# Gate and up projections in seven half-size products per pair, and the down projection in a stage of its own

## What is computed

```python
    x = x + gt1 * (merged @ w_out)                      # w_out 1024 x 1024
    h2 = rmsnorm(x, g_ffn) * (1 + sc2) + sh2            # sc2, sh2, gt2: one row per group of tokens
    gate, up = jnp.split(h2 @ w_gu, 2, axis=-1)         # w_gu 1024 x (2 * 2816)
    x = x + gt2 * ((jax.nn.silu(gate) * up) @ w_down)   # w_down 2816 x 1024
    return x, new_hist, C1, n1, m1
...
    y_prompt = rmsnorm(xp, g_final)
    y_sample = rmsnorm(xs, g_final)
```

## Time and profile before

| | us |
|---|---|
| median of 3 runs | 2039.96 (2039.92 to 2041.27) |
| the profiled execution | 2040.03 |
| its span, first to last instruction | 2038.3 |
| TensorE busy | 1975.2 (97%) |
| VectorE busy | 757.2 (37%) |
| ScalarE busy | 464.0 (23%) |
| GpSimd busy | 147.4 (7%) |
| DMA, mean | 99 GB/s |

### The profile page before, as it was taken

One profiled execution on the slowest core, in us unless ns is written; L12 is line 12 of the kernel. 1 busy time (PEld: TensorE's weight loads), 2 busy tenths in 40 slices (PEclk: granted clock), 3 DMA queues, 4 the chain that ended last, 5 costly groups with the idle time before them and its releaser, 6 DMA issues.

```text
span 2038.3 us, 28505 instructions
## 1 busy us (share of the span) xinstructions
PE 1975.2 (97%) x11613; PEld 1880.7 (92%) x11613; DVE 757.2 (37%) x1332; ACT 464.0 (23%) x656; POOL 147.4 (7%) x251
## 2 busy tenths in 40 slices
PE   7999999999999999999999969999999999999997
PEld 4899999999999987778999959999999999999997
DVE  5422213213333432334534554432442343344246
ACT  4232212223343342222202012111111111111113
POOL 0010029010000013210000011000000000000000
PEclk9999999999999999999999979999999999999999
DMA  8653335432434347445432311111111111111112
GB/s 284 240 170 114 120 109 163 145 112 77 117 100 123 102 144 166 134 143 186 152 98 65 101 36 32 42 52 41 41 41 51 41 41 41 43 50 41 41 52 88
DMA packets 224146, 200.84 MB, mean 99 GB/s; under 512 B 13251, under 2 KB 202487, under 8 KB 224079
## 3 DMA queue, kind: packets, MB, share of 16 engines
q1 hardware_dynamic: 214958, 166.31, 27.4%
q10 hardware_dynamic: 7721, 29.25, 3.6%
q0 software_dynamic: 1408, 4.46, 0.8%
HBM read 150.19 MB, written 49.92 MB: 98 GB/s over the span
## 4 chain that ended last, share of the span: by engine, by line
PE 94%; DVE 3%; ACT 1%; DMA 1%; issue 1%; SPq 0%; DVEq 0%; ACTq 0%
PE dense L1765 80%; PE misc L2075 2%; PE misc L2062 1%; PE misc L2001 1%; PE misc L2005 1%; PE misc L1974 1%; PE dense L1848 1%; PE misc L2003 1%; PE misc L1895 1%; PE misc L1894 1%; PE misc L1984 1%; DVE act_lo L1215 1%; PE misc L1848 1%; PE misc L2174 0%; DVE stage L1208 0%
## 5 line engine op out<-in xcount | busy, mean ns | idle before, releaser
L1765 PE MATMUL dense<-act_hi,w_hi 128*128 128x384 f32 (+1 forms) x2808 | 646.4, 338 | 19.7 <-DVE act_lo L1215 16.7
L1765 PE MATMUL dense<-act_lo,w_hi 128*128 128x384 f32 (+1 forms) x2808 | 622.1, 329 | 0.0
L1765 PE MATMUL dense<-act_hi,w_lo 128*128 128x384 f32 (+1 forms) x2808 | 621.0, 329 | 0.0
L1765 PEld LDWEIGHTS dense<-act_hi,w_hi 128*128 128x128 f32 x2808 | 481.1, 189 | 44.8 <-issue 27.7
L1765 PEld LDWEIGHTS dense<-act_hi,w_lo 128*128 128x128 f32 x2808 | 482.3, 189 | 0.0
L1765 PEld LDWEIGHTS dense<-act_lo,w_hi 128*128 128x128 f32 x2808 | 482.0, 189 | 0.0
L1200 DVE TENSOR_TENSOR w_lo<-raw,w_hi 128x1024 fp32r<-128x1024 f32 x139 | 173.0, 1245 | 464.5 <-ACT w_hi L821 463.7
L821 ACT ACTIVATE w_hi<-raw 128x1024 fp32r<-128x1024 f32 x139 | 146.9, 1058 | 397.9 <-PE dense L1765 395.7
L1697 DVE SCALAR_TENSOR_TENSOR hmT<-dense,mod,hmT 128x768 f32<-128x768 f32 x80 | 81.4, 1018 | 69.1 <-PE dense L1765 68.6
L926 ACT ACTIVATE stage<-dense 128x768 f32<-128x768 f32 x52 | 42.1, 810 | 285.1 <-PE dense L1765 285.0
L1765 PE MATMUL dense<-a_lo,w_hi 128*128 128x384 f32 (+1 forms) x480 | 106.3, 329 | 0.0
(11 more groups left out here) (302 smaller groups left out, 1486.7 us busy)
## 6 DMA issues: line engine op xcount, KB each, us to landing
z_scratch<-stage ACTq DMA_DIRECT2D x52, 544.0 KB, 2.7
raw<-in_w_in_dram SPq DMA_DIRECT2D x53, 512.0 KB, 3.8
ada_w<-in_w_ada_dram SPq DMA_DIRECT2D x24, 1024.0 KB, 5.5
raw<-in_w_gate_up_dram SPq DMA_DIRECT2D x44, 512.0 KB, 3.7
stage<-z_scratch SPq DMA_DIRECT2D x24, 544.0 KB, 3.6
raw<-in_w_down_dram SPq DMA_DIRECT2D x22, 512.0 KB, 3.5
qkv<-z_scratch SPq DMA_DIRECT2D x8, 1024.0 KB, 6.9
cs<-in_state_mlstm_c_dram SPq DMA_DIRECT2D x32, 256.0 KB, 5.3
```

What stands on the lines that cost most here:

```text
L1765: ins = pe.matmul(tile(k, c), w[:, n % 2, off:off + P], x[:, xr, t0:t1], start=(first and p == 0), stop=(last and p == 2))
```

## The change

**Gate and up.** The T = 1088 tokens are cut into two halves of TH = 544 (the second holds 480 prompt and the 64 sample tokens), the 1024 features into two halves of four tiles, and the output rows into gate and up. The product of these two by two blocks is made with seven products of half-size blocks (steps 0 to 6, STEPS), not eight, and 15 sums (Strassen's form in Winograd's variant): four of weight blocks (w_sums), four of activation blocks (combine, once for the whole stage), and the rest of results. Two hidden tiles are worked on together as a *pair*, 11 pairs (DUOS); each step has one product for each of the two tiles (q). A product is 4 feature tiles x 3 passes x 2 chunks of 272 columns = 24 matmuls, and a pair has 14. Two of the four sets of two PSUM banks serve a tile; steps 3 to 6 add onto what stands in the bank, and ScalarE copies out what other steps left (take_s1, take_s5, take_s2), VectorE adds to it (add_g1, add_g2, add_u2), and forms silu(gate) * up (gate2 for the second half of tokens, gate1 for the first). Weights are split by half blocks of 512 columns through a ring of four (w_high, w_low). The result is stored to DRAM (a_scratch, 22 x 544 KB).

**The norm** before it is made by token half. The last two units of the output projection run half by half; the first half's norm sums (col_sums, spread) stand between the second half's matmuls, the second half's between the first products of gate and up. GpSimd takes no part.

**Down** is a stage behind all of gate and up: six phases, for each token chunk (320, 384, 384) the first and the last 512 output features, in each 11 units of 24 matmuls over 256 hidden rows, into four banks. w_down is loaded and split three times over, through a ring of four (66 x 512 KB); the activations are loaded again from a_scratch and split, one chunk while the one before is used; x is stored to DRAM before the FFN and loaded again (8 x 544 KB) for the sum. The final norm goes by halves of 512 features.

The core of the diff:

```diff
+HT = 5
+KH = KT // 2
+KB = KH * P
+DUOS = FT // 2
+STEPS = 7
+DN, DQ = 2 * STEPS, 2
+IN_X, FRESH = (0, 3, 5, 6), (0, 1, 2)
+LOOP0, LOOPS = 3, 3
...
+        OPS = [tuple(blocks(ap) for ap in pair_) for pair_ in (
+            (first_op(0), first_op(1)), (first_op(2), first_op(3)), (half_op(2), half_op(3)), (half_op(0), half_op(1)),
+            (half_op(6), half_op(7)), (half_op(4), half_op(5)), (last_op[:, 0, :], last_op[:, 1, :]))]
...
+        def w_src(d, st, q):
+            g, u = raw_pair(d, q)
+            tmp = ssq[:, 0:KB] if d == 0 and q else s1b
+            return (g[:, 0:KB], g[:, KB:2 * KB], tmp, g[:, 0:KB], g[:, KB:2 * KB], u[:, 0:KB], u[:, KB:2 * KB])[st]
...
+        def p_banks(st, q):
+            return bank_pair(q if st in IN_X else 2 + q)
...
+            def gu_load(d, sem_, value, i=0):
+                for up in range(2):
+                    for q in range(2):
+                        src = gu_cols(d, q, up, i)
+                        if (up, q) == (0, 0):
+                            sp.wait_ge(sem_, value)
+                        sp.dma_start(raw_pair(d, q)[up].rearrange("p (k n) -> p k n", k=KT), src
+                                     ).then_inc(gu_in[(d - 1) % 2], 16)
+            def a_store(d, i=0):
+                for q in range(2):
+                    dst = a_rows(d, q, i)[:, TH:T]
+                    sp.wait_ge(a2_ready, at(d, DQ, q + 1, i))
+                    sp.dma_start(dst, sums[:, 2 + q, :]).then_inc(a2_out, 16)
+                for q in range(2):
+                    dst = a_rows(d, q, i)[:, 0:TH]
+                    sp.wait_ge(a1_ready, at(d, DQ, q + 1, i))
+                    sp.sem_inc(passed, 1)
+                    sp.dma_start(dst, set_sums(d, q)).then_inc(a1_out[d % 2], 16)
...
+                    if v == 3:
+                        sp.wait_ge(alo_ready, UNITS)
+                        sp.wait_ge(wlo_ready, DN * DUOS)
+                        for o in range(KT):
+                            sp.dma_start(hmT[:, o, :], z[Z_X + o]).then_inc(x1_in, 16)
...
+                if d or st > 2:
+                    act.wait_ge(p_done, at(d, DN, e - 3, i))
+                elif st:
+                    act.wait_ge(oh_full, 2 + st)
+                act.activation(w_ops(d, st, q)[0], w_src(d, st, q), ACT.Copy).then_inc(whi_ready, 1)
...
+            def take_s1(d, q, i=0):
+                act.wait_ge(p_done, at(d, DN, q + 1, i))
+                if d >= 2:
+                    act.wait_ge(a1_out[d % 2], i * 32 + 32 * (d // 2))
+                elif d:
+                    act.wait_ge(hlo_ready, HLO0 + 4 * KH)
+                act.activation(two(set_sums(d, q)), p_banks(0, q), ACT.Copy).then_inc(s1_ready, 1)
...
+            def w_sums(d, q, i=0, part=None):
+                g, u = raw_pair(d, q)
+                a11, a12, a21, a22 = g[:, 0:KB], g[:, KB:2 * KB], u[:, 0:KB], u[:, KB:2 * KB]
+                t = w_src(d, 2, q)
+                n = at(d, 8, 4 * q, i) if part is None else 3 * q
+                if part != 1:
+                    if part is None:
+                        dve.wait_ge(wlo_ready, at(d, DN, 4 + q, i))
+                    dve.tensor_tensor(t, a21, a22, ALU.add).then_inc(wsum_ready, 1)
+                    dve.wait_ge(wsum_ready, n + 1)
+                    dve.tensor_tensor(a21, a11, a21, ALU.subtract).then_inc(wsum_ready, 1)
+                    dve.wait_ge(wsum_ready, n + 2)
+                    dve.tensor_tensor(a11, t, a11, ALU.subtract).then_inc(wsum_ready, 1)
+                if part != 0:
+                    dve.wait_ge(wsum_ready, n + 3 if part is None else 6)
+                    dve.tensor_tensor(a12, a12, a11, ALU.subtract).then_inc(wsum_ready, 1)
...
+            def combine(st, kt):
+                first, second = hmT[:, kt, :], hmT[:, kt + KH, :]
+                dst, x, y = {2: (first[:, 0:TH], first[:, TH:T], first[:, 0:TH]), 3: (t2(kt), second[:, TH:T], first[:, 0:TH]),
+                             5: (first[:, TH:T], second[:, TH:T], first[:, TH:T]),
+                             6: (second[:, 0:TH], second[:, 0:TH], t2(kt))}[st]
+                if st < 4:
+                    dve.wait_ge(hs32_ready, HS0 + KT + KH * (st - 2) + kt + 1)
+                dve.tensor_tensor(dst, x, y, ALU.subtract).then_inc(hlo_ready, 1)
...
+            def add_g1(d, q, i=0):
+                dve.wait_ge(p_done, at(d, DN, DQ + q + 1, i))
+                dve.wait_ge(s1_ready, at(d, DQ, q + 1, i))
+                sa = two(set_sums(d, q))
+                dve.tensor_tensor(sa, p_banks(1, q), sa, ALU.add).then_inc(g1_ready, 1)
...
+            for k in range(6):
+                residual(k)
+            half_residual(6, 0)
+            for q in range(2):
+                w_low(0, 0, q)
+            half_residual(7, 0)
+            wait_full(dve, raw_in, U_FFN + 1, inc=16)
+            w_sums(0, 0, part=0)
+            half_diag(0)
+            dve.wait_ge(gu1_in, 32)
+            w_sums(0, 1, part=0)
+            half_residual(6, 1)
+            dve.wait_ge(rstd_ready, RSTD0 + 1)
+            dve.wait_ge(x1_out[0], 16 * KT)
+            for k in range(KH + 1):
+                if k < KH:
+                    norm_half(k, k, 0, TH)
+                if k:
+                    plain_low(k - 1)
+            for q in range(2):
+                w_low(0, 1, q)
+            half_residual(7, 1)
+            sum_h2(6)
+            sum_h2(7)
+            norm_half(4, 4, 0, TH)
+            norm_half(5, 5, 0, TH)
+            plain_low(4)
+            half_diag(1)
+            norm_half(6, 6, 0, TH)
+            plain_low(5)
+            norm_half(7, 7, 0, TH)
+            plain_low(6)
+            plain_low(7)
+            dve.wait_ge(wsum_ready, 6)
+            for q in range(2):
+                w_sums(0, q, part=1)
+            for q in range(2):
+                w_low(0, 2, q)
+            dve.wait_ge(rstd_ready, RSTD0 + 2)
+            dve.wait_ge(x1_out[1], 16 * 2)
...
+            made(2, add_g1s)
+            for q in range(2):
+                w_low(0, 3, q)
+            made(3)
+            for q in range(2):
+                w_low(0, 4, q)
+            made(4)
+            for q in range(2):
+                w_low(0, 5, q)
+            made(5)
+            for q in range(2):
+                add_g2(0, q)
+            for q in range(2):
+                w_low(0, 6, q)
+            made(6)
+            for q in range(2):
+                add_u2(0, q)
+            for q in range(2):
+                w_low(1, 0, q)
+            for q in range(2):
+                gate2(0, q)
+            gate1(0, 0)
...
+                gate1(d - 1, 1, i)
+                for q in range(2):
+                    w_low(d, 1, q, i)
+                w_sums(d, 0, i)
+                w_low(d, 2, 0, i)
+                w_sums(d, 1, i)
+                w_low(d, 2, 1, i)
+                add_g1(d, 0, i)
+                add_g1(d, 1, i)
+                for q in range(2):
+                    w_low(d, 3, q, i)
+                groups(0, 1)
+                for q in range(2):
+                    w_low(d, 4, q, i)
+                groups(2, 3)
+                for q in range(2):
+                    w_low(d, 5, q, i)
+                add_g2(d, 0, i)
+                add_g2(d, 1, i)
+                groups(4, 5)
+                for q in range(2):
+                    w_low(d, 6, q, i)
+                add_u2(d, 0, i)
+                add_u2(d, 1, i)
+                gate2(d, 0, i)
+                gate2(d, 1, i)
+                if not last:
+                    for q in range(2):
+                        w_low(d + 1, 0, q, i)
+                groups(6, 7)
+                gate1(d, 0, i)
...
-            pe.wait_ge(xsum_ready, 1)
-            col_sums(R_N2, ssq)
-            pe.wait_ge(diag_ready, 2)
-            sum_partitions(T_N2, sq)
...
+            wait_full(pe, round_free, R_NOUT)
+            half_unit(6, 0)
+            half_unit(7, 0)
+            half_unit(6, 1, 0, 4)
+            col_sums(0)
+            half_unit(6, 1, 4)
+            half_unit(7, 1, 0, 4)
+            spread(0)
+            half_unit(7, 1, 4)
+            def product(d, st, q, i=0):
+                pe.wait_ge(wlo_ready, at(d, DN, DQ * st + q + 1, i))
+                if d == 0 and st < 2:
+                    if st == 1 and q == 1:
+                        pe.wait_ge(rstd_ready, RSTD0 + 2)
+                    else:
+                        pe.wait_ge(oh_free, 2 + st * 2 + q)
+                elif st == 0:
+                    pe.wait_ge(a1_ready, at(d, DQ, q + 1 - DQ, i))
+                elif st == 1:
+                    pe.wait_ge(g2_ready, at(d, DQ, q + 1 - DQ, i))
+                else:
+                    pe.wait_ge((g1_ready, s1_ready, s5_ready, s2_ready, u2_ready)[st - 2], at(d, DQ, q + 1, i))
+                (w1, w2), (x1, x2) = w_ops(d, st, q), OPS[st]
+                out = p_banks(st, q)
+                for kt in range(KH):
+                    if d == 0 and q == 0:
```

(77 more changed lines are left out.)

986 lines of the change are left out of this document (639 added, 347 removed).

## The result

| | before | after |
|---|---|---|
| median of 4 runs, us | 2040.62 (2039.92 to 2041.46) | 2017.6 (2015.99 to 2020.13) |
| the profiled execution, us | 2040.03 | 2019.2 |
| its span, us | 2038.3 | 2017.5 |

The ratio is 0.9888, interval 0.9871 to 0.9905: the change makes the kernel 23 us (1.1%) faster, not the 61 us of the forecast, and the time lies above the range (1960 to 2004). The profiled execution's span is 40.1 us above the forecast's 1977.4.

The account below looks back on a forecast made before the run. TensorE was taken as the bound, never idle in the steady part. First pair's end 1273.4 + ten pairs 420.7 + down 2.2 + 263.6 + 6.5 + end 11.0 = 1977.4 us span, plus 1.7: 1979 us; range 1960 to 2004.

Parts of the forecast that it names:

- The price of a 272-column matmul: TensorE, gate and up: 125.2 ns each, from trace rows at 256, 320 and 384 columns; ends 124.0 and 128.
- N / 2.4 + 2.5: Rival on matmul time: 115.8 ns at 272 columns, 9.4 ns less for each of 3888 matmuls, 1942 us; chance 0.02.
- the one with 146 ns: Rival: a 272-column matmul takes as long as one of 320 (146.1 ns), 77 us more, 2056 us; chance 0.01.
- Gate and up: Gate and up: 3696 matmuls at 125.2 ns, 462.7 us where 527.2 stood; 42.1 us a pair, saving 64.5 us.
- I take no wait: Said twice: no wait at steady pairs' bank hand-overs (1.8 to 2.2 us spare), none for SP's loads in down.
- each pair waits: Rival: late PSUM bank hand-overs at add_g1, gate1 and add_u2 add 7 us a pair, 2049 us; chance 0.05.
- Into the FFN: Output projection's end through the first pair: VectorE's queue bounds it, 62.7 us plus 11.6 of waits; pair ends at 1273.4.
- The rival of a longer first pair: First pair: the clock stays at its lower level for most of it, about 18 us more, 1997 us; chance 0.12.
- Down: Down stage: 1584 matmuls 263.6 us, 60 transposes 6.5, handover 2.2; splits hidden, loads on SP's queue without a wait.
- the ring lets a load be about 20 us late: SP's queue in down: a load may be about 20 us late before TensorE stops; reloads hold the queue 14 to 18.
- down waits for DMA: Rival: at 200 GB/s on the one load queue, down's phases 0 and 1 take 51 us, not 39: 2003 us; chance 0.10.
- w_hi late in the first two phases: Sign that the forecast is wrong: DMA at its limit in down's first two phases, with w_hi late.

Follow-up runs that it names:

- experiment 6: Kernel with experiment 2's swap and add_u2 first in the first pair; in pairs 1 to 9 add_u2 and gate2 moved behind the next pair's first low parts: 1990.32 us.
- experiment 2: The change with two statements swapped on SyncE's queue in phases 1 and 3, weight load ahead of activation load: 1971.13 us, ratio 0.9661.
- Experiments 4 and 5: 4: add_u2 ahead of step 6's operands in the first pair, on experiment 2: 1968.59 us. 5: on that, eight first-pair differences moved to GpSimd: 1969.03 us.
- experiment 3: The change with its order and waits kept, but activation loads of phases 1 and 3 bring 16 of 384 columns: 2011.03 us, ratio 0.9854.

## Why the prediction was right or wrong

- **What bounds the kernel now:** right. TensorE sets gate and up, and in steady pairs it is never idle.
- **The price of a 272-column matmul:** 125.2 ns forecast, 124.8 measured (2725 in 340.00 us). The interpolation between 256 and 384 columns holds. At N / 2.4 + 2.5 it would be 115.8: that rival is refuted, and so is the one with 146 ns. The Trainium skill (TensorE: Matmul & The Clock Gate, Back-to-back issue gap) gives this formula for a single matmul by itself, not for a stream of them as here.
- **Gate and up:** 420.7 us for ten pairs, 419.8 measured; VectorE 22.2 us a pair forecast and 21.4 measured (172.96 in 8.1 pairs), ScalarE 15.4 and 14.1. "I take no wait" was right, and experiment 6 shows that the room at add_u2 is as small as it was said to be. The rival "each pair waits" didn't occur.
- **Into the FFN:** step 6 at 1264.4 forecast, 1262.22 measured; the pair's end 1273.4 and 1270.9; 7 us of waiting before step 6 and 5.9 measured. Part of this closeness is luck. VectorE had the first half's 1/rms at 1194.0, 3.9 us later than forecast, because the sixth output unit, ahead of the change, ended at 1170.0 and not at 1166.0 (why is open). From there step 6 came after 68.2 us and not 74.3: VectorE was busy for 57.7 of them, forecast 62.7, and without work for 10.5, forecast 11.6. So the term was some 6 us too long, and in the kernel of experiment 2, which starts the stretch 3.7 us earlier, the pair ends at 1266.3: that is most of the 8 us by which its 1971 lies below the forecast's 1979. The step itself was slow as forecast: 8.7 us for its two products, where the forecast had 9. TensorE's loss is about 33 us (from about 1196, where its work on the output projection ends, to 1270.9, less 42.1), 39 forecast and 35.6 before: the early start is taken back by VectorE's queue. Experiments 4 and 5 bear out that queue as the cause. The rival of a longer first pair didn't occur: the clock was 0.89 from 1187 to 1264.
- **Down:** wrong, and the whole of the error. The step is the one on "SP's queue", which ends in "I take no wait". It counted the bytes (260 GB/s) and the depth of the ring (about 20 us), and neither was what held the stage: with the two statements swapped, the stage takes 271.8 us for 272.3 forecast, at 227 GB/s in phase 1. The step that failed is "the ring lets a load be about 20 us late": that is so only if the wait ahead of a load is for that load's own buffer. In its place the runs show one load in flight and 7.7 us a unit in two of the six phases, 316.7 us for the stage. The prediction walked the queues of VectorE and ScalarE instruction by instruction and SyncE's only as a sum of bytes, though the sequencer meets waits in order like any other. The numbers for it were at hand: 3.5 us to land, 1.06 and 1.22 for the two splits, the prediction's own 0.95 for the low part, and 0.4 for an issue make 7.1 us a turn (7.7 measured, where a load lands in 4.1) against 3.5 and 4.2, in some 8 turns of each of two phases, less what the ring had in store.
- **The rival "down waits for DMA"** named the right stage at 2003, with a wrong mechanism. The measured DMA rate in the waiting phases is low (135 and 117 GB/s) because loads are issued late; experiment 3 leaves about 5 us of 44 to the bytes.
- **What would show it:** "w_hi late in the first two phases" was to be the sign of a DMA at its limit. It came in the second and the fourth phase, with DMA at 0.42 and 0.36: the busy share beside the wait told the two causes apart at once.
- **The end:** 11.0 forecast, 10.1 measured.

## What to carry to other kernels

Walk a queue that only issues transfers like any other engine: for each wait on it, ask which loads stand behind, and whether what ends the wait needs one of them. Two rings on one queue, where a load of one waits for a consumer that stands behind the other ring's consumer, make a circle with one load in flight, however many buffers there are; its sign is idle time on TensorE and a low DMA share together, and its period is the landing plus every split on the way. Put the load whose data is wanted first ahead of the wait that can be late.

## What the runs showed of the hardware

Subtractions with both operands in SBUF, 544 columns of float32, take 0.72 us on VectorE alone, and 1.8 us on VectorE and 1.8 on GpSimd side by side, so that 5.7 us of work given to GpSimd cost VectorE 8.8. One on each engine every 1.8 us looks like work by turns; how long one takes on GpSimd alone was not measured. The Trainium skill (SBUF — State Buffer, Who interferes with whom) states that a VectorE instruction with two SBUF inputs contends with a GpSimd instruction that reads SBUF, and that the later one blocks; the trace agrees, as far as VectorE's instructions get longer exactly while GpSimd's run. That such an exchange can cost VectorE more time than it frees stood in the expectation only as its second rival.

In the phases in which TensorE stopped every few microseconds the granted clock was 0.83 and 0.97 in the mean, between its two levels of 1.2 and 2.4 GHz; with the stops gone it is 1.00 in the same phases (experiment 2). Most of the slower matmuls are no loss of their own, since each turn's length is set by the load and the splits; those behind the last turn of each waiting phase are, some 4 us in all.
